# Delta rule's q, k, v projection: ten of twelve pairs of channel tiles by seven block products in place of eight, with one turning buffer

## Chip, cores and metric

One core of a Trainium2 chip runs the kernel. The metric is its device time in microseconds, the median of several executions. The other numbers come from one profiled execution of the kernel before.

## The reference

A decoder trunk of two layers over 1024 tokens of width 1024, in float32. The even layer has retention and dilated attention, the odd layer a gated delta rule; each is followed by a layer norm, a convolutional feed-forward net and another layer norm. What concerns the change is the head of the odd layer's mixer:

```python
def _odd_mixer(x, w_in, conv_w, a_log, dt_bias, norm_w, w_out):
    hproj = x @ w_in
    qkv = jax.nn.silu(_causal_dwconv(hproj[..., :3 * GDN_W], conv_w))
    gate = hproj[..., 3 * GDN_W:4 * GDN_W]
```

`3 * GDN_W` is 3072 channels: 24 tiles of 128, of which the first eight are q, then eight k, then eight v, one head each. The convolution has four taps along the tokens. The sums of squares of q and k over a head's channels are wanted later, for their lengths.

## The kernel before

All engines have queues of their own, and the order in each is written out by hand; semaphores join them. The stages follow one another on the core: `project_out` "ffn0_down" (the feed-forward net's second projection, its layer norm, and x turned to channel-major), `conv_tokens` "odd_qkv" (the stage that is changed), `project_tokens` "odd_gate", then the delta rule. Between stages all engines meet at a barrier.

**Arithmetic.** Operands are float32 numbers split in a high part (a cast, on ScalarE) and a low part (a subtraction, on VectorE). A product is three matmuls per 128 rows of contraction: high by high, high by low, low by high. x lies split in SBUF as `xhi` and `xlo`, 128 partitions by 8 channel chunks by 1024 tokens.

**`conv_tokens`, line 1834.** For each of 24 tiles, `products` (line 1881) makes 8 chunks x 3 matmuls x 2 halves of the tokens, 48 matmuls of 128x512 (line 1890), into one of two PSUM buffers. ScalarE scales the result by the last tap (line 1936), VectorE adds the other three taps straight from PSUM (line 1964), ScalarE takes the silu (line 1942). SyncE stores q and k tiles channel-major in `feat`. TensorE turns the tile by eight transposes (line 1905) into one of two turning buffers in PSUM. From there ScalarE sums the squares of q and k tiles (line 1918, eight activations) and copies k and v tiles out (line 1925) and stores them in `kv`. TensorE's queue has tile j+1's products ahead of tile j's turn. ScalarE's order for a tile is last tap, high part of tile j+2's weights (line 1914), silu, squares, copy; VectorE's is three taps, low part of tile j+2's weights (line 1955). For the last tiles `following.split_hi` and `split_lo` prepare the first weights of the gate projection.

**`ffn_up`, line 327.** The feed-forward net's first projection already works in pairs of tiles (the gate's and the value's), with 22 pairs. The first two (`PLAIN`) are made by whole products (line 470). For the other 20 the 2x2 blocks of a pair's weights (two tiles by two halves of the contraction) and of x (two halves of the contraction by two halves of the tokens) are combined so that seven block products are enough in place of eight: `product` (line 507), 12 matmuls each. VectorE makes four sums of weight blocks (`add_sources`, lines 628 to 633), ScalarE and VectorE split seven weight blocks (lines 548 and 639), and seven sums of results (lines 647 to 680) give the pair's 2x2 blocks. For this, three differences of x's blocks are made and split at the start of the stage (lines 602 to 618), and the fourth takes the place of a quarter of x in `xhi` and `xlo`. They are made from the unsplit x, which `project_out` leaves when it is given `raw` (`keep_raw`, line 890).

## Time and profile before

| | us |
|---|---|
| median of 3 runs (3083.44 to 3085.64) | 3084.43 |
| profiled execution, its own time | 3084.53 |
| its span, first to last instruction | 3082.7 |
| TensorE busy (matmuls) | 2871.6 (93%) |
| VectorE busy | 1726.1 (56%) |
| ScalarE busy | 1171.7 (38%) |
| GpSimd busy | 392.0 (13%) |
[...]

The busy shares are means over stages of different kinds. The stage that is changed runs from its first matmul at 1556.88 us to the next stage's first at 1856.22 us. In timelines a matmul's start is exact and its end modelled, so the spacing of starts tells what a matmul costs; 512 columns last 0.39 us each and follow one another faster than that. [...] In square brackets stands how long the engine had been idle before an instruction and what released it.

### The profile page before, as it was taken

How to read it: one execution, taken by the hardware profiler on the slowest of the kernel's cores; microseconds unless marked ns; L12 is line 12 of the kernel's file. 1: busy time of each engine (PE TensorE's matmuls, PEld its weight loads, DVE VectorE, ACT ScalarE, POOL GpSimd, SP SyncE). 2: the span in 40 equal slices, each digit the busy share in tenths (PEclk: the TensorE clock that was granted, in tenths of full speed). 3: DMA queues.
4: the chain of work that ended last, by engine and by line, in shares of the span. 5: the costliest groups of instructions: out<-in, count | busy, mean ns of one | idle time of the engine just before them, and what ended most of it. 6: DMA issues, size and time to landing. Idle time of an engine off the chain costs nothing. (4 is left out here: it accounts for less than half of the span.)

```text
span 3082.7 us, 45826 instructions
## 1 busy us (share of the span) xinstructions
PE 2871.6 (93%) x17734; PEld 2419.6 (78%) x17734; DVE 1726.1 (56%) x2736; ACT 1171.7 (38%) x2046; POOL 392.0 (13%) x337
## 2 busy tenths in 40 slices
PE   8999967979899999999989989799987999999996
PEld 6888856877778888788778876699976888887885
DVE  4111125674769999736544442255538799996363
ACT  3211124752344444322334532355434444443221
POOL 0000046330100000000010001255412000000002
PEclk9999988999999999999989999899998999999998
DMA  4322143425222222354322422432032222224443
GB/s 166 103 88 95 68 153 112 115 71 184 96 84 89 82 84 86 144 179 145 131 105 96 132 67 77 168 104 92 16 137 101 79 82 85 87 82 181 143 143 126
DMA packets 149994, 337.59 MB, mean 110 GB/s; under 512 B 36096, under 2 KB 70080, under 8 KB 139328
## 3 DMA queue, kind: packets, MB, share of 16 engines
q1 hardware_dynamic: 119632, 297.43, 28.4%
q10 hardware_dynamic: 30192, 37.82, 3.6%
q8 instruction: 116, 1.90, 0.3%
q14 instruction: 54, 0.44, 0.0%
HBM read 251.12 MB, written 84.05 MB: 109 GB/s over the span
## 5 line engine op out<-in xcount | busy, mean ns | idle before, releaser
L308 PE MATMUL even_in_acc<-even_in_w_hi,even_x_hi 128*128 128x512 f32 x576 | 224.9, 390 | 13.5 <-DVE even_x_lo L266 13.5
L309 PE MATMUL even_in_acc<-even_in_w_lo,even_x_hi 128*128 128x512 f32 x576 | 224.8, 390 | 0.0
L310 PE MATMUL even_in_acc<-even_in_w_hi,even_x_lo 128*128 128x512 f32 x576 | 224.8, 390 | 0.0
L272 DVE TENSOR_TENSOR even_in_w_lo<-even_in_w_raw,even_in_w_hi 128x512 fp32r<-128x512 f32 x72 | 49.6, 691 | 291.3 <-ACT even_in_w_hi L229 291.3
L1964 DVE SCALAR_TENSOR_TENSOR odd_qkv_conv<-odd_qkv_acc,odd_qkv_taps,odd_qkv_conv 128x1023 f32<-128x1023 f32 (+2 forms) x72 | 92.3, 1282 | 172.4 <-ACT odd_qkv_conv L1936 170.6
L958 DVE TENSOR_TENSOR ffn_a_lo<-ffn_a_raw,ffn_a_hi 128x512 fp32r<-128x512 f32 x84 | 58.0, 691 | 229.8 <-ACT ffn_a_hi L879 229.8
L1041 POOL TENSOR_SCALAR ffn_down_rstd<-ffn_down_mean_var 128x1 f32<-128x1 f32 x16 | 6.0, 374 | 1347.1 <-DVE ffn_down_mean_var L976 1347.1
L879 ACT CAST ffn_a_hi<-ffn_a_raw 128x512 fp32r<-128x512 f32 x84 | 52.3, 623 | 321.7 <-PE ffn_down_acc L921 310.5
L308 PEld LDWEIGHTS even_in_acc<-even_in_w_hi,even_x_hi 128*128 128x128 f32 x576 | 108.6, 189 | 35.9 <-issue 13.4
L310 PEld LDWEIGHTS even_in_acc<-even_in_w_hi,even_x_lo 128*128 128x128 f32 x576 | 108.5, 188 | 22.8
L309 PEld LDWEIGHTS even_in_acc<-even_in_w_lo,even_x_hi 128*128 128x128 f32 x576 | 108.5, 188 | 22.5
L1890 PE MATMUL odd_qkv_acc<-odd_x_hi,one_hi 128*128 128x512 f32 x384 | 121.2, 397 | 3.8 <-PEq L64 3.8
L1890 PE MATMUL odd_qkv_acc<-odd_x_lo,one_hi 128*128 128x512 f32 x384 | 119.0, 391 | 0.0
L1890 PE MATMUL odd_qkv_acc<-odd_x_hi,one_lo 128*128 128x512 f32 x384 | 118.8, 391 | 0.0
L921 PE MATMUL ffn_down_acc<-two_hi,ffn_a_hi 128*128 128x512 f32 x352 | 108.5, 390 | 3.5 <-DVEq L952 2.7
L921 PE MATMUL ffn_down_acc<-four_hi,ffn_a_hi 128*128 128x512 f32 x352 | 108.8, 391 | 2.7 <-DVEq L952 2.7
L921 PE MATMUL ffn_down_acc<-four_hi,ffn_a_lo 128*128 128x512 f32 x352 | 109.2, 392 | 0.0
L921 PE MATMUL ffn_down_acc<-four_lo,ffn_a_hi 128*128 128x512 f32 x352 | 108.9, 391 | 0.0
L921 PE MATMUL ffn_down_acc<-two_hi,ffn_a_lo 128*128 128x512 f32 x352 | 108.4, 389 | 0.0
L921 PE MATMUL ffn_down_acc<-two_lo,ffn_a_hi 128*128 128x512 f32 x352 | 108.4, 389 | 0.0
L239 ACT ACTIVATE even_in_stage<-even_in_acc 128x2048 f32<-128x2048 f32 x18 | 33.8, 1879 | 175.3 <-PE even_in_acc L310 175.3
L229 ACT CAST even_in_w_hi<-even_in_w_raw 128x512 fp32r<-128x512 f32 x72 | 44.7, 623 | 125.2 <-PE even_in_acc L310 117.7
(503 smaller groups left out, 7962.7 us busy)
## 6 DMA issues: line engine op xcount, KB each, us to landing
ffn_w_raw<-in_ffn_up SPq DMA_DIRECT2D x42, 1024.0 KB, 4.9
ffn_down_w_raw<-in_ffn_down SPq DMA_DIRECT2D x84, 512.0 KB, 3.7
ffn_a_raw<-hidden SPq DMA_DIRECT2D x88, 256.0 KB, 3.8
even_in_w_raw<-in_ev_w_in SPq DMA_DIRECT2D x18, 1024.0 KB, 5.6
hp<-even_in_stage ACTq DMA_DIRECT2D x18, 1024.0 KB, 4.2
even_out_w_raw<-in_ev_w_out SPq DMA_DIRECT2D x24, 512.0 KB, 3.6
hidden<-even_mixed SPq DMA_DIRECT2D x22, 512.0 KB, 2.6
odd_qkv_w_raw<-in_od_w_qkv SPq DMA_DIRECT2D x22, 512.0 KB, 4.3
```

The lines of the kernel that those rows point to most:

```text
L229: act.copy(at(w_hi, k), w_raw[:, k]).then_inc(hi_ready, 1)
L239: act.activation(stage[:, h], acc[:, h], func).then_inc(acc_free, 1)
L272: dve.tensor_tensor(at(w_lo, k), w_raw[:, k], f32(at(w_hi, k)), ALU.subtract).then_inc(lo_ready, 1)
L308: pe.matmul(acc[:, h, t], xhi[:, k, tok], at(w_hi, k), start=(k == 0), stop=False)
L309: pe.matmul(acc[:, h, t], xhi[:, k, tok], at(w_lo, k), start=False, stop=False)
L310: mm = pe.matmul(acc[:, h, t], xlo[:, k, tok], at(w_hi, k), start=False, stop=(k == KD - 1))
L879: act.copy(a_hi[:, s], a_part(2 * i + s, s, hf)).then_inc(hi_ready, 1)
L921: mm = pe.matmul(acc[:, t, n], aa[:, s, tok], ww[:, s, n * NB:(n + 1) * NB], start=(opening and aa is a_hi and ww is w_hi), stop=(last and ...
L958: dve.tensor_tensor(a_lo[:, s], a_part(k, s, hf), f32(a_hi[:, s]), ALU.subtract).then_inc(lo_ready, 1)
L1041: pool.tensor_scalar(rstd[:, t], mean_var[:, t, 1:2], EPS, None, ALU.add).then_inc(rstd_ready, 1)
L1890: mm = pe.matmul(acc[:, s, tok], ww[:, s, k], xx[:, k, tok], start=(k == 0 and ww is w_hi and xx is xhi), stop=(k == KD - 1 and ww is w_lo))
L1964: dve.scalar_tensor_tensor(out=conv[:, s, back:SEQ], in0=acc[:, s, 0:SEQ - back], scalar=tap(j, GDN_CONV - 1 - back), in1=conv[:, s, back: ...
```

## The change

`conv_tokens` takes over the scheme of `ffn_up`. The 24 tiles form 12 pairs; the first two pairs are made by whole products (192 matmuls), the other ten by seven block products (84 matmuls each in place of 96). The results are collected in SBUF (`c`), and the taps read them there. Six PSUM banks hold results, two hold the only turning buffer, so that a tile is turned when the tile before has been squared and copied out. The first projection's end keeps the unsplit x (`raw`), and conv, rows, c and the weight sums lie in its place later. One quarter of x is overwritten by a difference; it is stored in HBM at the start (`quarter`), loaded again after the last weights are split, and split anew for the gate projection. The gate's first weights are loaded late, into place `one`. The closing of the outer scope (`ctx.close()`) moves behind the stage. `split_hi`, `split_lo`, `add_sources`, `keep_first` and the `add_` functions are as in `ffn_up`, but that the last sum of u reuses the second's buffer.

```diff
--- before.py
+++ after.py
-def conv_tokens(nc, name, xhi, xlo, w, taps_dram, ident, n_tiles, feat, out, sumsq, first, place, following):
+def conv_tokens(nc, name, xhi, xlo, x_raw, w_raw, w, taps_dram, ident, n_tiles, feat, out, sumsq, first, places, following, quarter):
...
+    KH = KD // 2
+    PLAIN = 2
+    ORDER = 7
+    BANKS = 6
+    PAIRS = n_tiles // 2
+    W = PAIRS - PLAIN
+    LAST = PAIRS - 1
+    SUMMED = (2, 1, 3)
...
+        c, conv, rows = (x_raw[:, 2 * n:2 * n + 2] for n in range(3))
+        rows = rows.rearrange("p s (t n) -> p s t n", n=P)
+        sums = x_raw[:, 6:8].rearrange("p a (k n) -> p (a k) n", n=P).rearrange("p (i k) n -> p i k n", k=KH)
+        t_hi = sc.sbuf("t_hi", [P, 3, KH, HALF], F32R)
+        t_lo = sc.sbuf("t_lo", [P, 3, KH, HALF], F32R)
+        u1, u2, u4 = (sc.sbuf(f"u{n}", [P, HALF]) for n in (1, 2, 4))
...
-        acc = sc.psum("acc", [P, 2, SEQ])
-        turn = sc.psum("turn", [P, 2, TT, P])
+        bank = sc.psum("acc", [P, BANKS, HALF])
+        turn = sc.psum("turn", [P, TT, P])
...
+        def source(m, i):
+
+            raw = w_raw[:, m % 2]
+            return (raw[:, 0, chunks[0]], sums[:, 1], sums[:, 0], sums[:, 2], raw[:, 0, chunks[1]], sums[:, 3],
+                    raw[:, 1, chunks[1]])[i]
+
+        def operand(i):
+
+            def quarter(k, t):
+                return [x[:, chunks[k], toks[t]] for x in (xhi, xlo)]
+
+            def difference(n):
+                return [x[:, n] for x in (t_hi, t_lo)]
+
+            return (quarter(0, 0), difference(0), quarter(0, 1), difference(1), quarter(1, 0), quarter(1, 1), difference(2))[i]
+
...
+            sp.dma_start(quarter, x_raw[:, chunks[0], toks[1]]).then_inc(quarter_stored, 16)
+            load_raw(1)
             sp.dma_start(taps[:], taps_dram).then_inc(taps_in, 16)
+            load_raw(2)
+            sp.wait_ge(first_lo, 3)
+            load_raw(3)
+            for j in range(2):
+                store_feat(j)
+            for m in range(W):
+                for j in range(2 * m + 2, 2 * m + 4):
+                    store_feat(j)
+                if m + 2 < W:
+                    sp.wait_ge(lo_done, ORDER * (m + 1))
+                    load_raw(m + 4)
+            sp.wait_ge(lo_done, ORDER * W)
+            sp.wait_ge(quarter_stored, 16)
+            sp.dma_start(again, quarter).then_inc(quarter_in, 16)
+            sp.wait_ge(prod_done, ORDER * (W - 1) + 3)
+            following.load(sp)
...
+            def product(m, i):
+                pe.wait_ge(lo_done, ORDER * m + i + 1)
+                if m == 0 and i < 6:
+                    pe.wait_ge(evicted, (2, 2, 3, 3, 4, 4)[i])
+                if m > 0 and i == 0:
+                    pe.wait_ge(u2_done, m)
+                if m > 0 and i == 1:
+                    pe.wait_ge(u4_done, m)
+                if m > 0 and i == 2:
+                    pe.wait_ge(c22_done, m)
+                    pe.wait_ge(u3_done, m)
+                if m > 0 and i == 3:
+                    pe.wait_ge(c11_done, m)
+                if m > 0 and i == 4:
+                    pe.wait_ge(c12_done, m)
+                if m > 0 and i == 5:
+                    pe.wait_ge(c21_done, m)
+                if i == 6:
+                    pe.wait_ge(u1_done, m + 1)
...
+                hi, lo = operand(i)
+                for k in range(KH):
+                    for n, (ww, xx) in enumerate(((slot(0, i), hi), (slot(0, i), lo), (slot(1, i), hi))):
+                        mm = pe.matmul(result(m, i), ww[:, k], xx[:, k], start=(k == 0 and n == 0), stop=(k == KH - 1 and n == 2))
                 mm.then_inc(prod_done, 1)
...
+            def turn_tile(j):
                 pe.wait_ge(silu_done, j + 1)
-                if j > 1:
-                    pe.wait_ge(squared, TT * min(j - 1, QK))
-                if j - 2 >= Q:
-                    pe.wait_ge(copied, j - 1 - Q)
+                if j > 0:
+                    pe.wait_ge(squared, TT * min(j, QK))
...
+            low, high = range(KH), range(KH, KD)
+            pe.wait_ge(first_lo, 2)
+            for g in range(2):
+                for f in range(2):
+                    mm = whole_part(0, g, f, range(KD), True, True)
+                mm.then_inc(whole_done, 1)
+            pe.wait_ge(first_lo, 3)
+            whole_part(1, 0, 1, low, True, False)
+            whole_part(1, 0, 0, range(KD), True, True)
+            mm = whole_part(1, 0, 1, high, False, True)
+            mm.then_inc(whole_done, 1)
+            pe.wait_ge(evicted, 1)
+            mm = whole_part(1, 1, 1, low, True, False)
+            mm.then_inc(early_done, 1)
+            whole_part(1, 1, 0, range(KD), True, True)
+            mm = whole_part(1, 1, 1, high, False, True)
+            mm.then_inc(whole_done, 1)
+            turn_tile(0)
+            for m in range(W):
+                for i in range(ORDER):
+                    product(m, i)
+                    if m == 0 and i == 1:
+                        turn_tile(1)
+                    if i == (3 if m == 0 else 2):
+                        turn_tile(2 * m + 2)
+                    if i == 5:
+                        turn_tile(2 * m + 3)
+            for g in range(2):
+                turn_tile(2 * LAST + g)
...
+            def evict(j, g):
+                act.wait_ge(whole_done, 2 * j + g + 1)
+                if j == 0:
+                    act.wait_ge(t_lo_done, 3 * KH)
+                else:
+                    act.wait_ge(taps_done, g + 1)
+                act.copy(c[:, g], bank[:, (4 * j + 2 * g) % BANKS:(4 * j + 2 * g) % BANKS + 2].rearrange("p f t -> p (f t)")
...
+            def last_tap(j, g):
+                tile = 2 * j + g
+                if j < PLAIN:
+                    act.wait_ge(evicted, tile + 1)
+                elif g == 0:
+                    act.wait_ge(c11_done, j - PLAIN + 1)
+                    act.wait_ge(c12_done, j - PLAIN + 1)
+                else:
+                    act.wait_ge(c22_done, j - PLAIN + 1)
+                    act.wait_ge(c21_done, j - PLAIN + 1)
+                if j > 0:
+                    act.wait_ge(turned, tile - 1)
+                    act.wait_ge(feat_stored[g], 16 * min(j, QK // 2))
+                act.activation(conv[:, g], c[:, g], ACT.Copy, scale=tap(tile, GDN_CONV - 1)).then_inc(tap_done, 1)
+
+            def silu(tile):
+                act.wait_ge(taps_done, tile + 1)
+                act.activation(conv[:, tile % 2], conv[:, tile % 2], ACT.Silu).then_inc(silu_done, 1)
+
+            def take_rows(tile):
+                act.wait_ge(turned, tile + 1)
+                if tile < QK:
+                    for t in range(TT):
+                        act.activation(squares[:, t], turn[:, t], ACT.Square, accum_out=sumsq[:, t, tile:tile + 1]
+                                       ).then_inc(squared, 1)
+                    act.wait_ge(squared, TT * (tile + 1))
+                if tile >= Q:
+                    s, i = tile % 2, tile - Q
+                    act.wait_ge(stored[s], 16 * (i // 2))
+                    act.copy(rows[:, s], turn[:]).then_inc(copied, 1)
+                    act.wait_ge(copied, i + 1)
+                    act.dma_start(out[:, :, i * P:(i + 1) * P].rearrange("t p n -> p t n"), rows[:, s]).then_inc(stored[s], 16)
...
+            for g in range(2):
+                evict(0, g)
+            for g in range(2):
+                last_tap(0, g)
+            for g in range(2):
+                silu(g)
+            evict(1, 0)
+            act.wait_ge(early_done, 1)
+            for k in range(KH):
+                first_difference_hi(k)
+            for i in range(3):
+                split_hi(0, i)
+            evict(1, 1)
+            for i in range(3, ORDER):
+                split_hi(0, i)
+            take_rows(0)
+            last_tap(1, 0)
+            for m in range(W):
+                more = m + 1 < W
+                tile = 2 * m + 2
+                keep_first(m)
+                if m == 0:
+                    take_rows(1)
+                    last_tap(1, 1)
+                if more:
+                    split_hi(m + 1, 0)
+                silu(tile)
+                if more:
+                    for i in range(1, 3):
+                        split_hi(m + 1, i)
+                take_rows(tile)
+                if more:
+                    split_hi(m + 1, 3)
+                silu(tile + 1)
+                if more:
+                    split_hi(m + 1, 4)
+                else:
+                    act.wait_ge(quarter_in, 16)
+                    act.wait_ge(prod_done, ORDER * m + 3)
+                    act.copy(xhi[:, chunks[0], toks[1]], again).then_inc(quarter_hi, 1)
                     following.split_hi(act)
-                act.wait_ge(acc_free, j + 1)
-                act.activation(conv[:, s], conv[:, s], ACT.Silu).then_inc(silu_done, 1)
-                act.wait_ge(turned, j + 1)
-                if j < QK:
-                    square_rows(j)
-                if j >= Q:
-                    copy_out(j)
+                last_tap(m + PLAIN, 0)
+                if more:
+                    split_hi(m + 1, 5)
+                take_rows(tile + 1)
+                if more:
+                    split_hi(m + 1, 6)
+                last_tap(m + PLAIN, 1)
+            for g in range(2):
+                silu(2 * LAST + g)
...
+            dve.wait_ge(quarter_stored, 16)
+            differences(0)
+            for k in range(1, KH):
+                differences(k)
+                differences_lo(k - 1)
+                if k == 2:
+                    dve.wait_ge(first_hi, 3)
+                    dve.tensor_tensor(whole_lo[1], w_raw[:, 1], f32(whole_hi[1]), ALU.subtract).then_inc(first_lo, 1)
+            differences_lo(KH - 1)
+            dve.wait_ge(taps_in, 16)
+            for g in range(2):
+                other_taps(g)
+            for k in range(KH):
+                first_difference_lo(k)
+            split_lo(0, 0)
+            add_sources(0)
+            for i in range(1, ORDER):
+                split_lo(0, i)
+            for m in range(W):
+                more = m + 1 < W
+                tile = 2 * m + 2
+                if more:
+                    add_sources(m + 1)
+                other_taps(tile)
+                add_u2(m)
+                if more:
+                    split_lo(m + 1, 0)
+                add_u4(m)
+                if more:
+                    split_lo(m + 1, 1)
+                other_taps(tile + 1)
+                add_c22(m)
+                add_u3(m)
+                if more:
+                    split_lo(m + 1, 2)
+                    split_lo(m + 1, 3)
+                add_c11(m)
+                add_c12(m)
+                if more:
+                    split_lo(m + 1, 4)
+                    split_lo(m + 1, 5)
+                else:
+                    dve.wait_ge(quarter_hi, 1)
+                    dve.tensor_tensor(xlo[:, chunks[0], toks[1]], again, f32(xhi[:, chunks[0], toks[1]]), ALU.subtract)
                     following.split_lo(dve)
+                add_c21(m)
+                if more:
+                    split_lo(m + 1, 6)
+            for g in range(2):
...
+    quarter = dram("quarter", [P, KD // 2, HALF])
...
-            gate_first = Ahead(top, "odd_gate", two, KD // 2,
+            gate_first = Ahead(top, "odd_gate", one, KD // 2,
                                [t["od_w_gate"][0, :, 0:KD // 2].rearrange("p k n -> p (k n)")], 2)
             project_out(nc, "ffn0_down", None, KF, k_rows(t["ffn_down0"]), x1, t["ln2_g"][0:1], t["ln2_b"][0:1],
                         ident, x2, x2_hi, x2_lo, place=two, first=down_first, following=qkv_first,
-                        rows=rows, a_stored=h_stored[0], lead=rest)
+                        rows=rows, a_stored=h_stored[0], lead=rest, raw=mixed[:, 0:KD])
+            conv_tokens(nc, "odd_qkv", x2_hi, x2_lo, mixed[:, 0:KD], w_raw, t["od_w_qkv"], t["od_taps"], ident, 3 * GDN_W // P,
+                        feat, kv, sumsq, qkv_first, (one, two), gate_first, quarter)
             ctx.close()
-            conv_tokens(nc, "odd_qkv", x2_hi, x2_lo, t["od_w_qkv"], t["od_taps"], ident, 3 * GDN_W // P, feat, kv, sumsq,
-                        qkv_first, one, gate_first)
             project_tokens(nc, "odd_gate", x2_hi, x2_lo, t["od_w_gate"], GDN_W // NB, gate, None,
                            lambda sc, lent: project_decay(sc, lent, x2_hi, x2_lo, t["od_w_ba"], t["od_a_log"],
                                                           t["od_dt_bias"], upper, ident, gates, sumsq, gc_rows),
-                           ACT.Silu, gate_stored, gate_first, (two, one))
+                           ACT.Silu, gate_stored, gate_first, (one, two))
         places_ctx.close()
 
         one = weight_place(top_ctx, "three")

```

## Rows read from the trace of the kernel before

**Rows 1.** Stretches: us, busy time of each engine, TensorE's granted clock, DMA share, GB/s

```profile
1563.00:1640.00 77.00, 77.00 (x365) 64.19 (x364) 29.87 (x24) 29.58 (x98) 0.00 (x0) 1.00 0.24 83
```

**Rows 2.** Timeline of TensorE in the stage: start us, duration us, engine, line, operation

```profile
1640.10 0.71 PE L1890 MATMUL odd_qkv_acc<-odd_x_hi,one_hi 128*128 128x512 f32 x2
...
1651.87 0.70 PE L1890 MATMUL odd_qkv_acc<-odd_x_hi,one_hi 128*128 128x512 f32 x2
```

**Rows 3.** Timeline of TensorE, two products of a pair in the feed-forward stage

```profile
1000.54 0.39 PE L507 MATMUL ffn_up_tiles_acc<-ffn_x_hi,two_hi 128*128 128x512 f32 x1
...
1003.26 0.39 PE L507 MATMUL ffn_up_tiles_acc<-ffn_up_tiles_t_hi,two_hi 128*128 128x512 f32 x1
```

**Rows 4.** Timeline of VectorE, feed-forward stage, then the taps in the changed stage

```profile
1000.74 0.69 DVE L680 TENSOR_TENSOR even_mixed<-ffn_up_tiles_acc,ffn_up_tiles_u 128x512 f32<-128x512 f32 x1 [0.83 <-PE ffn_up_tiles_acc L507]
1001.40 0.69 DVE L639 TENSOR_TENSOR one_lo<-ffn_w_raw,one_hi 128x512 fp32r<-128x512 f32 x1
1002.01 0.69 DVE L628 TENSOR_TENSOR even_mixed<-ffn_w_raw 128x512 f32<-128x512 f32 x1
...
1004.54 1.27 DVE L423 SCALAR_TENSOR_TENSOR even_mixed<-even_mixed,ffn_up_taps 128x1023 f32<-128x1023 f32 x1
...
1643.74 3.92 DVE L1964 SCALAR_TENSOR_TENSOR odd_qkv_conv<-odd_qkv_acc,odd_qkv_taps,odd_qkv_conv 128x1023 f32<-128x1023 f32 x3 [6.75 <-ACT odd_qkv_conv L1936]
```

**Rows 5.** Timeline of ScalarE, feed-forward stage, then silu and a k tile's rows

```profile
908.73 0.61 ACT L548 CAST one_hi<-even_mixed 128x512 fp32r<-128x512 f32 x1
909.24 0.62 ACT L548 CAST one_hi<-ffn_w_raw 128x512 fp32r<-128x512 f32 x1
...
1001.52 1.24 ACT L414 ACTIVATE even_mixed<-even_mixed,ffn_up_taps 128x1024 f32<-128x1024 f32 x1 [0.15 <-DVE even_mixed L680]
...
1647.69 1.06 ACT L1942 ACTIVATE odd_qkv_conv<-odd_qkv_conv 128x1024 f32<-128x1024 f32 x1 [3.05 <-DVE odd_qkv_conv L1964]
...
1699.31 0.28 ACT L1918 ACTIVATE odd_qkv_squares<-odd_qkv_turn 128x128 f32<-128x128 f32 x1 [1.56 <-PE odd_qkv_turn L1905]
...
1701.52 1.02 ACT L1925 COPY odd_qkv_rows<-odd_qkv_turn 128x1024 f32<-128x1024 f32 x1
...
1703.06 1.12 ACT L1936 ACTIVATE odd_qkv_conv<-odd_qkv_acc,odd_qkv_taps 128x1024 f32<-128x1024 f32 x1 [0.52 <-ACT odd_qkv_rows L1925]
```

**Rows 6.** Timeline of TensorE, from first turn to the next stage, with and without keep_raw

```profile
831.73 2.78 PE L947 MATMUL even_out_acc<-top_ident,even_out_y 128*128 128x128 f32 x24
...
859.73 0.76 PE L470 MATMUL ffn_up_tiles_acc<-ffn_x_hi,two_hi 128*128 128x512 f32 x1 [4.23 <-PEq L64]
...
1529.60 2.79 PE L947 MATMUL ffn_down_acc<-top_ident,ffn_down_y 128*128 128x128 f32 x24
...
1556.88 1.19 PE L1890 MATMUL odd_qkv_acc<-odd_x_hi,one_hi 128*128 128x512 f32 x2 [3.77 <-PEq L64]
```

**Rows 7.** DMA issues of the page: line, count, KB each, us from issue to landing

```profile
hp<-even_in_stage ACTq DMA_DIRECT2D x18, 1024.0 KB, 4.2
```

**Rows 8.** Instructions of line 507: count, ns min/median/max, first and last start

```profile
L507 PEld LDWEIGHTS ffn_up_tiles_acc<-ffn_x_hi,two_hi x160: 187/188/188, 905.1 to 1274.4; 128*128 128x128 f32 x160
```

**Rows 9.** Timeline of TensorE, the end of the stage

```profile
1839.72 1.04 PE L1905 MATMUL odd_qkv_turn<-top_ident,odd_qkv_conv 128*128 128x128 f32 x8
1848.53 1.97 PE L1905 MATMUL odd_qkv_turn<-top_ident,odd_qkv_conv 128*128 128x128 f32 x8 [7.78 <-ACT odd_qkv_conv L1942]
1856.22 0.76 PE L308 MATMUL odd_gate_acc<-two_hi,odd_x_hi 128*128 128x512 f32 x1 [5.72 <-DVEq L276]
```

**Rows 10.** Matmuls after gaps (TensorE's timeline), and one stretch as in group 1

```profile
673.48 1.06 PE L1664 MATMUL dil_bank<-top_ident,dil_probs 128*128 128x128 f32 x8 [1.19 <-ACT dil_probs_t L1715]
...
1288.95 0.70 PE L921 MATMUL ffn_down_acc<-two_hi,ffn_a_hi 128*128 128x512 f32 x2 [2.65 <-DVEq L952]
...
2815.40 0.70 PE L921 MATMUL ffn_down_acc<-four_hi,ffn_a_hi 128*128 128x512 f32 x2 [2.70 <-DVEq L952]
...
2818.00:2820.00 2.00, 2.00 (x6) 1.55 (x6) 2.00 (x2) 0.77 (x1) 0.00 (x0) 0.56 0.94 307
```

224 lines of the change are left out of this document (151 added, 73 removed).

## The prediction

> **What bounds the kernel now.** I read the stretches first, to see whether the stage that is edited is held by TensorE. It is: TensorE is busy in all 77.00 us of the stretch, at a granted clock of 1.00, while VectorE and ScalarE are busy for 30 us each [rows 1]. Then the order in time. One tile of the projection takes 11.77 us from its first product to the next tile's (1640.10 to 1651.87) [rows 2]. Forty-eight matmuls of 128x512 fill most of it; the feed-forward stage, which already uses seven block products, shows their spacing: 12 in 2.72 us (1000.54 to 1003.26), 0.2267 us each [rows 3]. That makes 10.88 us, and leaves 0.89 us for the tile's eight transposes. So matmuls that are taken out here are worth their full time, as long as the other two engines keep up. The profiled execution took 3084.53 us (span 3082.7); the sum is made against that, 0.1 us above the median of 3084.43.
>
> **What is removed.** Ten pairs go from 96 matmuls to 84. A pair then takes 84 x 0.2267 + 2 x 0.89 = 20.82 us of TensorE in place of 23.54 [rows 2, 3]: 2.72 us a pair, 27.2 us in all, if nothing waits.
>
> **What VectorE gets.** A pair costs it: six taps, 2 x 3.83 us (three in 3.92 us; the last overlaps its successor) [rows 4]; four sums of weights, 2.53 us (1002.01 to 1004.54); seven low parts and seven sums of results at about 0.61 us (1001.40 to 1002.01), 8.5 us. Together 18.7 of 20.82 us. It is not the bound by its sum. The order in its queue is another matter.
>
> **The walk through one pair.** Let T be the start of a pair's first product. Products are 2.72 us, so TensorE wants the first of the pair's two turns (the transposes of one tile) after three of them, at T+8.16. That turn waits for the tile's silu, which waits for its taps, which stand in VectorE's queue behind the four sums of the next weights, which stand behind the last low part of the pair's own weights, and this waits for ScalarE's last high part. In the feed-forward stage that high part comes at once. Here `take_rows` of the other tile stands ahead of it, and with one turning buffer that tile is turned only after the sixth product.
> From the end of the sixth product of the pair before, then: results are visible 0.20 us later (1000.54 to 1000.74), their sum takes 0.69, and ScalarE starts the tap 0.09 us after its end (1001.52) [rows 4, 5]. On ScalarE: tap 1.14 us (it lasts 1.24, and overlaps its successor by 0.1 as the high parts do, 0.61 long and 0.51 apart), high part 0.52 [rows 5], `take_rows`, last high part 0.62 and 0.04 to VectorE. `take_rows` is 2.21 us for q tiles (squares, 1699.31 to 1701.52), 1.54 for v tiles (copy, and its store's issue, to 1703.06), 3.75 for k tiles, which do both [rows 5]. On VectorE: low part 0.61, sums 2.53, taps 3.92 [rows 4]; silu 1.09 with its start, 0.05 to TensorE. Without `take_rows` that is 0.98+1.14+0.52+0.66+0.61+2.53+3.92+1.14 = 11.50 us. TensorE has 0.89+2.72+8.16 = 11.77 us of own work between the same two points (one turn, the seventh product, three products). So the wait of the first turn is `take_rows` minus 0.27: 1.9 us after a q tile, 3.5 after a k tile, 1.3 after a v tile. It recurs in each pair, since the chain starts from TensorE's own sixth product and so moves with the wait.
> Now count. The second to the tenth pair have this chain. The second starts behind a fuller VectorE: in the first pair two tiles' taps follow each other late (the walk from the head gives its last low part at T+3.15 in place of T+1.9, a wait of 3.1). The third and fourth follow q tiles (2 x 1.9), the fifth to eighth k tiles (4 x 3.5), the ninth a v tile (1.3); the tenth has no next weights to sum, its taps begin 2.5 us sooner, no wait. Sum: **22.2 us** given back of 27.2. A pair behind a k tile takes 24.3 us, more than the 23.54 of before.
>
> **Head.** `keep_raw` adds eight copies out of PSUM on ScalarE to the end of the projection before, and TensorE's last turns wait for them. From the first turn to the next stage's first matmul it took 27.28 us without them (1529.60 to 1556.88) and 28.00 with them (831.73 to 859.73): +0.7 [rows 6]. Closing the outer scope, which moves behind the stage, I take as 0.6 at the end, bounds 0 and 1.5.
> The store of x's quarter is new and VectorE's first difference waits for it. It is 1024 KB; such a store took 4.2 us to land [rows 7]. SyncE's queue has the weights of the second pair behind it, which are needed only after TensorE's first 96 matmuls, over 20 us later. All of VectorE's and ScalarE's head moves by some 5 us. In the walk the differences end at 25 us, silu of the second tile at 37, when TensorE is at 37 itself; the second weights of the first seven-product pair are split at 44.4 and wanted at 48.9. So the store costs nothing with 4.5 us to spare. Its bounds are 0 and the 5 us of it that are not covered if it lands twice as late.
> The four plain tiles took 45.4 us in the feed-forward stage (859.73 to 905.1) [rows 6, 8], the slow first matmuls included; same work here. One turn (0.89), then the first pair with three turns, 21.71.
>
> **Tail.** Now 16.50 us pass from the last product's end to the next stage's first matmul (1839.72 to 1856.22) [rows 9]. After: both last tiles must be tapped, silued, turned at the slow rate (1.97 us for eight, row 1848.53) and copied one after the other, 4.6 us for store and barrier as now. What VectorE does ahead: the quarter's low part (128x2048, about 2.2 us) and the next weights' low parts (4 x 0.61) stand before the last sum, which starts 1.7 us late. Then 7.8 us of taps, silu 1.1, turn 2.0, copy 1.0: 19.8 us, +3.3. The quarter's load is issued at T+1.5 of the last pair and read at T+14, so it is hidden.
>
> **Sum.** Stage after: 45.4 + 0.9 + 21.7 + 9 x 20.82 + 22.2 + 19.8 + 0.6 = 298.0 us; before 1556.88 to 1856.22, 299.3; with 0.7 at the head the change is **-0.6 us**.
>
> **The clock.** What is new is that TensorE stands still in the middle of dense matmuls, for 2.9 us once, 3.3 us four times (the wait less the 0.16 us in which the last matmul drains). The trace has few such gaps: 2.65 us was followed by full speed (two matmuls in 0.70, then pairs 0.54 apart), 2.70 us by a clock of 0.56 in the stretch 2.6 us later, and 1.19 by full speed [rows 10]. The two rows near 2.7 are the same place in the two layers, the start of the down projection, and went both ways; 3.3 is longer than either. Bounds for one gap: nothing, and 1.9 us, which is what the slow start of the feed-forward stage cost (45.4 us for 192 matmuls that make 43.5 at 0.2267). I take 1.5 for each of the five: **+7.5 us**. The waits after q tiles (gap 1.75) lie between 1.19 and 2.65: 0 each, up to 1.7.
> [...]
> So 3084.53 - 0.6 + 7.5 = 3091.4 us.
>
> **Rivals.** What a measurement can tell from no change is 0.2%, 6.2 us.
> A, the walk with the clock falling: 3091.4, from 3087 to 3095. Chance 0.50.
> B, the walk, and the clock holds or falls while the engine stands anyway: -0.6, some 3084. For it the 2.65 us row [rows 10], against it the 2.70 us row. 0.15.
> C, ScalarE's and VectorE's chain is shorter than the walk (an order that I read too strictly, steps that overlap more), and the silus come in time: -0.6 - 22.2 = -22.8, some 3062. For it: both engines have time to spare by their sums; against: every step has its row and the queues run in order. 0.15.
> D, slower: the clock falls at every wait of the first turn, and and stays down twice as long behind the k tiles, where the engine stands longest. 3 x 1.7 for the q and v waits, 4 x 1.9 more for the k waits: 3104. It decides if the gap of 1.75 us is enough; nothing between 1.19 and 2.65 in my rows says no. 0.20.
> That the matmuls do not become fewer can be excluded: the loops give 192 + 840 in place of 1152.
>
> **Numbers.** A lies about the bound of 3090.6: 0.32 slower, 0.18 same. B: 0.12 same, 0.03 faster. C faster, D slower. Faster 0.18, same 0.30, slower 0.52. The range reaches from below B, a third of the way to C, to near D: 3074 to 3103.
>
> **What would show it.** In the changed profile: 84 matmuls and two turns in 20.8 us where nothing waits; TensorE idle ahead of the first turn of pairs two to nine, released by ScalarE's silu, longest behind k tiles; VectorE's last low part released by ScalarE, not by TensorE; a granted clock under 1 several times in the stage. Wrong would be: no idle before the turns (C), or a clock of 1.00 throughout (B), or a first seven-product pair that waits for VectorE's splits (the store is not hidden).

## The result and the profile after

The changed kernel takes 3092.98 us (median of 13 runs, 3089.28 to 3097.37), the kernel before, beside it, 3085.37 us (13 runs, 3082.09 to 3092.2): ratio 1.0024, 95% interval 1.0015 to 1.0032. It is slower, by a little more than the 0.2% that the prediction took as the least that can be told from no change. Its profiled execution took 3092.21 us, with a span of 3090.4. Of the 7.7 us by which that span is longer, the profile has 1.0 ahead of the stage, 3.8 in it, and 2.9 behind it, in code that is the same.

The page of the changed kernel, busy time of each engine:

```profile
span 3090.4 us, 46057 instructions
PE 2853.5 (92%) x17614; PEld 2401.6 (78%) x17614; DVE 1836.2 (59%) x2928; ACT 1216.8 (39%) x2134; POOL 393.4 (13%) x337
```

TensorE has 120 matmuls fewer and is busy 18.1 us less, but VectorE works 110 us more and ScalarE 45. The same stretch as in [rows 1], after:

```profile
1563.00:1640.00 77.00, 74.17 (x342) 61.66 (x341) 66.06 (x87) 45.75 (x123) 0.00 (x0) 0.98 0.24 89
```

VectorE was busy for 29.87 of 77 us and now is for 66.06. The stage is no longer TensorE's alone: TensorE idles in it, and its granted clock (a share of full speed, the mean over the stretch) is 0.98 in place of 1.00. Where it idles stands in its timeline. These rows are the first turn of the projection before, the stage's first matmul, its first turn, and then turns before which TensorE waited, two of them with the pair's other turn below:

```profile
1529.72 2.78 PE L947 MATMUL ffn_down_acc<-top_ident,ffn_down_y 128*128 128x128 f32 x24
...
1557.86 0.76 PE L1959 MATMUL odd_qkv_acc<-odd_x_hi,one_hi 128*128 128x512 f32 x1 [4.35 <-PEq L64]
...
1603.15 1.03 PE L2000 MATMUL odd_qkv_turn<-top_ident,even_mixed 128*128 128x128 f32 x8
...
1636.98 1.97 PE L2000 MATMUL odd_qkv_turn<-top_ident,even_mixed 128*128 128x128 f32 x8 [2.83 <-ACT even_mixed L2086]
...
1661.09 1.09 PE L2000 MATMUL odd_qkv_turn<-top_ident,even_mixed 128*128 128x128 f32 x8 [1.65 <-ACT even_mixed L2086]
...
1708.03 1.92 PE L2000 MATMUL odd_qkv_turn<-top_ident,even_mixed 128*128 128x128 f32 x8 [3.14 <-ACT even_mixed L2086]
...
1733.83 1.09 PE L2000 MATMUL odd_qkv_turn<-top_ident,even_mixed 128*128 128x128 f32 x8 [3.09 <-ACT even_mixed L2086]
1742.95 1.03 PE L2000 MATMUL odd_qkv_turn<-top_ident,even_mixed 128*128 128x128 f32 x8
...
1758.00 1.09 PE L2000 MATMUL odd_qkv_turn<-top_ident,even_mixed 128*128 128x128 f32 x8 [3.12 <-ACT even_mixed L2086]
1768.75 1.04 PE L2000 MATMUL odd_qkv_turn<-top_ident,even_mixed 128*128 128x128 f32 x8
...
1848.13 1.97 PE L2000 MATMUL odd_qkv_turn<-top_ident,even_mixed 128*128 128x128 f32 x8 [7.27 <-ACT even_mixed L2086]
...
1860.99 0.77 PE L308 MATMUL odd_gate_acc<-one_hi,odd_x_hi 128*128 128x512 f32 x1 [6.32 <-DVEq L276]
```

The seven-product pairs wait 2.83 us once, 1.65 and 1.67 behind q tiles, 3.14, 3.09, 3.12 and 3.12 behind k tiles, 0.89 behind a v tile, and the last not at all. Each wait is released by ScalarE's silu (line 2086). A clock that fell can be read off the rows without a view of the clock: from the waiting turn to the pair's other turn it is 9.12 us after the 3.09 us gap (1733.83 to 1742.95) and 10.75 after the next (1758.00 to 1768.75), for the same work. The stretches of 4 us behind three of these turns have it as a granted clock of 0.57, 1.00 and 0.67:

```profile
1708.00:1712.00 4.00, 3.97 (x15) 3.49 (x16) 3.93 (x6) 3.02 (x18) 0.00 (x0) 0.57 0.34 135
1733.00:1737.00 4.00, 3.17 (x18) 2.80 (x19) 3.96 (x6) 3.85 (x19) 0.00 (x0) 1.00 0.35 135
1758.00:1762.00 4.00, 4.00 (x16) 3.32 (x17) 3.93 (x6) 3.81 (x19) 0.00 (x0) 0.67 0.33 131
```

And this is the chain behind one such wait, ScalarE first, then VectorE (a high part and then the eight squares of the k tile stand where ScalarE's first "..." is):

```profile
1719.75 1.15 ACT L2082 ACTIVATE even_mixed<-even_mixed,odd_qkv_taps 128x1024 f32<-128x1024 f32 x1 [2.87 <-DVE even_mixed L2236]
...
1723.52 1.02 ACT L2098 COPY even_mixed<-odd_qkv_turn 128x1024 f32<-128x1024 f32 x1
1724.57 0.37 ACTq L2100 DMA_DIRECT2D kv<-even_mixed  x1
1724.98 0.62 ACT L2061 CAST two_hi<-ffn_w_raw 128x512 fp32r<-128x512 f32 x1 [0.44 <-ACT even_mixed L2098]
...
1732.72 1.06 ACT L2086 ACTIVATE even_mixed<-even_mixed 128x1024 f32<-128x1024 f32 x1 [5.08 <-DVE even_mixed L2249]
```

```profile
1718.98 0.69 DVE L2236 TENSOR_TENSOR even_mixed<-odd_qkv_acc,odd_qkv_u 128x512 f32<-128x512 f32 x1 [2.03 <-PE odd_qkv_acc L1990]
...
1725.63 0.69 DVE L2203 TENSOR_TENSOR two_lo<-ffn_w_raw,two_hi 128x512 fp32r<-128x512 f32 x1 [2.32 <-ACT two_hi L2061]
1726.24 0.69 DVE L2192 TENSOR_TENSOR even_mixed<-ffn_w_raw 128x512 f32<-128x512 f32 x1
...
1728.77 3.91 DVE L2249 SCALAR_TENSOR_TENSOR even_mixed<-even_mixed,odd_qkv_taps 128x1023 f32<-128x1023 f32 x3
```

The other tile's rows hold ScalarE from 1721.32 to 1724.94, so the last high part comes at 1724.98; VectorE waits 2.32 us for it, then sums the next weights, and only then taps the tile that TensorE wants. The changed kernel run again on another chip gave the same picture.

> The changed kernel once more, for the comparisons of this call. About 1.0024 of the kernel before (some 7.6 us over it). Walk: the eight waits before a pair's first turn come again, 20.8 us in all, 1.8 us after q tiles and 3.3 us after k tiles; the clock falls after some of the gaps of about 3 us, not the same ones each time, so single times differ by multiples of some 1.5 us.

Measured: 3092.7 us, ratio 1.0020 (1.0011 to 1.0029). The waits are 2.83, 1.66, 1.66, 3.13, 3.09, 3.12, 3.12 and 0.91 us, within 0.02 us of the first profile; the clock fell after three of the five long ones, not after four (the granted clock of the 4 us from the turn is 0.59, 0.57 and 0.65 after the three, 1.00 after the other two).

### The profile page after: what moved, and what is told of

The parts are those of the page before. It is cut to its first block and busy times, and to the rows that moved or that the text cites. A ratio compares the mean times of both kernels' runs of the same rounds, so it can differ in the third digit from the quotient of the medians.

```text
span 3090.4 us, 46057 instructions
## 1 busy us (share of the span) xinstructions
PE 2853.5 (92%) x17614; PEld 2401.6 (78%) x17614; DVE 1836.2 (59%) x2928; ACT 1216.8 (39%) x2134; POOL 393.4 (13%) x337
## 5 line engine op out<-in xcount | busy, mean ns | idle before, releaser
L2249 DVE SCALAR_TENSOR_TENSOR even_mixed<-even_mixed,odd_qkv_taps 128x1023 f32<-128x1023 f32 (+2 forms) x72 | 92.1, 1281 | 4.9 <-ACT even_mixed L2082 3.2
L921 PEld LDWEIGHTS ffn_down_acc<-two_hi,ffn_a_hi 128*128 128x128 f32 x352 | 66.5, 189 | 19.1 <-DVEq L952 3.0
L921 PEld LDWEIGHTS ffn_down_acc<-four_hi,ffn_a_hi 128*128 128x128 f32 x352 | 66.5, 189 | 17.3 <-DVEq L952 3.3
L2676 PE MATMUL gdn_bank<-gdn_xt_blk,gdn_t_m 64*64 64x64 f32 x1280 | 78.7, 221 | 0.8 <-DVE gdn_t_m L2913 0.8
```

What stands on the lines that cost most here:

```text
L921: mm = pe.matmul(acc[:, t, n], aa[:, s, tok], ww[:, s, n * NB:(n + 1) * NB], start=(opening and aa is a_hi and ww is w_hi), stop=(last and ...
L2249: dve.scalar_tensor_tensor(out=conv[:, g, back:SEQ], in0=c[:, g, 0:SEQ - back], scalar=tap(tile, GDN_CONV - 1 - back), in1=conv[:, g, back ...
L2676: pe.matmul(d_ps[q][half, h % HG], t_m[half, h], xt_blk[half, s, h], start=True, stop=True)
```

## The experiments

**The chain, cut on ScalarE.**

```diff
-                take_rows(tile + 1)
                 if more:
                     split_hi(m + 1, 6)
+                take_rows(tile + 1)
```

> ScalarE makes the last high part of the next weights before it takes the other tile's rows out of the turning buffer. Walk (the rows stand ahead of that high part, and so ahead of VectorE's sums, taps and the silu): the wait before the first turn becomes the same after q, k and v tiles, 0.9 us each (1.6 for the second pair), 7.9 us in all in place of 20.8; no gap is over 2 us, so the clock stays at full speed: about 19 us under the changed kernel, some 3074. Rival 1, the single turning buffer holds TensorE: rows are taken out later than before, so the same or longer, 3093 or more. Rival 2, VectorE is short of time as a whole (18.7 of 20.8 us): within 3 us of 3093.

Measured: 3075.63 us, ratio 0.9959 (0.9945 to 0.9972). The wait behind a k tile in this kernel's timeline:

```profile
1703.69 1.09 PE L2000 MATMUL odd_qkv_turn<-top_ident,even_mixed 128*128 128x128 f32 x8 [0.73 <-ACT even_mixed L2086]
```

The waits are 1.47 us once and then 0.73 or 0.74 seven times, behind q, k and v tiles alike, and the clock fell nowhere between the head and the tail (granted 1.00 from 1610 to 1824 us). So what made the waits differ by kind of tile was `take_rows` ahead of the last high part. One swap takes the ratio from 1.0020, on the same chip, to 0.9959: the gaps add up to 6.6 us in place of 19.5, and the falls of the clock are gone as well.

**The chain, cut on VectorE.**

```diff
-                if more:
-                    add_sources(m + 1)
                 other_taps(tile)
+                if more:
+                    add_sources(m + 1)
```

> VectorE adds the first tile's taps before it sums the next pair's weight blocks. Walk: the chain to the silu is 2.5 us shorter; waits only in the second pair (0.6 us) and the four pairs behind k tiles (0.8 each), 3.8 us in all in place of 20.8, no fall of the clock: about 23 us under the changed kernel, some 3070. Rival 1, the single turning buffer: no difference, since the rows are taken out at the same time. Rival 2, VectorE short of time: no difference, since its work is the same.

Measured: 3078.81 us, ratio 0.9975 (0.9966 to 0.9985): faster, but 9 us short of the expectation. The waits are 1.23 (new: the first pair's second turn), 0.85, 0.55, 0.54, 2.01, 2.00, 2.00 and 0.59 us. VectorE's timeline in a pair of k tiles shows why:

```profile
1690.50 0.68 DVE L2236 TENSOR_TENSOR even_mixed<-odd_qkv_acc,odd_qkv_u 128x512 f32<-128x512 f32 x1
...
1697.15 0.69 DVE L2203 TENSOR_TENSOR two_lo<-ffn_w_raw,two_hi 128x512 fp32r<-128x512 f32 x1 [2.90 <-ACT two_hi L2061]
1697.76 3.92 DVE L2249 SCALAR_TENSOR_TENSOR even_mixed<-even_mixed,odd_qkv_taps 128x1023 f32<-128x1023 f32 x3
1701.59 0.69 DVE L2192 TENSOR_TENSOR even_mixed<-ffn_w_raw 128x512 f32<-128x512 f32 x1
```

I had taken 2.5 us off each wait. But the four sums are only moved: they now stand between the taps and the sixth result's sum (line 2236), which starts straight behind its predecessor, held by VectorE, where it had waited 2.03 us for TensorE. The chain starts later, and `take_rows` is still in it (2.90 us for the high part). The clock fell after one of the three gaps of 2.0 us (granted 0.58 in the 4 us from the turn, 1.00 after the other two), and here that was nearly free: the wait after it is 0.59 us in place of 2.00, and from this waiting turn to the next it is 23.27 us against 23.06 without a fall.

**Both cuts.**

> Both orders together. Walk: no wait before any turn, TensorE without a gap from the stage's first product to the last pair's end; 20.8 us and the clock's 6 us come back: about 27 us under the changed kernel, some 3066, 0.6% under the kernel before. Rival 1 and rival 2: as with one order alone, 3090 or more.

Measured: 3068.28 us, ratio 0.9936 (0.9922 to 0.9949). From the second pair on no turn waits. The middle of the stage, this kernel first and the changed one below it:

```profile
1642.00:1820.00 178.00, 174.63 (x839) 145.55 (x837) 157.74 (x199) 112.49 (x290) 0.00 (x0) 1.00 0.39 128
```

```profile
1642.00:1820.00 178.00, 161.32 (x746) 132.98 (x745) 137.64 (x177) 100.19 (x277) 0.00 (x0) 0.97 0.32 107
```

In 178 us there are 839 matmul records instead of 746, at a clock of 1.00 instead of 0.97. The stage takes 277.7 us in place of 303.1: the 25.4 us between them are the 20.8 of waits and some 6 of clock, less the 1.21 us that the first pair's second turn now waits.

**The clock apart from the wait.** Eleven extra matmuls, whose results nobody reads, fill most of each of the five long gaps (m = 1, 4, 5, 6, 7):

```diff
+                    if i == 2 and m in (1, 4, 5, 6, 7):
+                        pe.wait_ge(lo_done, ORDER * m + 4)
+                        pe.wait_ge(c11_done, m)
+                        for _ in range(11):
+                            pe.matmul(result(m, 3), slot(0, 3)[:, 0], operand(3)[0][:, 0], start=True, stop=True)
                     if i == (3 if m == 0 else 2):
                         turn_tile(2 * m + 2)
```

> As the changed kernel, but in the five pairs with a gap of about 3 us (the second, the fifth to eighth) TensorE fills the wait before the first turn with 11 matmuls of 128x512 whose results the next product overwrites: 2.5 us of work, done before the silu comes. Walk and clock: the turns start when they did, the eight waits cost the same 20.8 us, but the granted clock stays at 1.00 from the stage's first turn to its last pair, which takes away three or four falls of 1.6 us: 5 to 6 us under the changed kernel, some 3087. Rival: the clock falls for another reason (the load of the whole kernel), and then the falls stay, and the time is 3093; or the added matmuls delay the turns, and then it is above.

Measured: 3088.19 us, ratio 1.0011 (1.0001 to 1.0020).

```profile
1703.39 2.65 PE L2030 MATMUL odd_qkv_acc<-odd_qkv_t_hi,two_hi 128*128 128x512 f32 x11
1706.68 1.09 PE L2000 MATMUL odd_qkv_turn<-top_ident,even_mixed 128*128 128x128 f32 x8 [0.63 <-ACT even_mixed L2091]
```

The eleven take 2.65 us, the turn comes when it did, and the k pairs still follow each other at 24.17 us. Four gaps of 0.62 or 0.63 and one of 0.35 are left, and the granted clock is 1.00 from 1610 to 1835 us. The stage is 5.3 us shorter (297.8 against 303.1). Its first turn comes 0.7 us later here than in the changed kernel (46.0 us into the stage against 45.3), and from that turn on it is 6.0 us shorter, as much as the four falls cost by the rows. Idling thus cost the waits themselves and, on top, some 6 us of clock: the two terms are separate, as the sum had them.

**The quarter of x.** Its store, its load and its new split are left out here, so the gate projection reads the difference in that quarter's place:

```diff
-            sp.dma_start(quarter, x_raw[:, chunks[0], toks[1]]).then_inc(quarter_stored, 16)
...
-            sp.dma_start(again, quarter).then_inc(quarter_in, 16)
...
-                    act.copy(xhi[:, chunks[0], toks[1]], again).then_inc(quarter_hi, 1)
...
-            dve.wait_ge(quarter_stored, 16)
...
-                    dve.wait_ge(quarter_hi, 1)
-                    dve.tensor_tensor(xlo[:, chunks[0], toks[1]], again, f32(xhi[:, chunks[0], toks[1]]), ALU.subtract)
```

> Leaves out that x's quarter is stored, loaded again and split again, so the gate projection works on a wrong quarter of x. Walk: VectorE starts its differences 7.5 us sooner, and no product starts sooner for it (0 us in the stage's head); at the end VectorE's last sum starts as soon as TensorE's last product is done, and the two last tiles come 1.7 us sooner: 3091, 2 us under the changed kernel. Rival: the store holds up the head, and then the first turn or the first products of the first seven-product pair come sooner too, by up to 5 us: 3086.

Measured: 3090.78 us, ratio 1.0021 (1.0012 to 1.0031). In the changed kernel VectorE's first difference waits for the store:

```profile
1563.37 0.69 DVE L2167 TENSOR_TENSOR even_mixed<-even_mixed 128x512 f32<-128x512 f32 x1 [7.55 <-DMA quarter<-even_mixed]
```

Here it starts 5.5 us after the stage's first matmul (1557.86), without the store at once (1560.19, where the first matmul starts too). Yet the first turn that waits comes 79.1 us into the stage with the store (1636.98) and 78.9 without: hidden. At the tail the last tiles' first turn waits 5.70 us in place of 7.27, which looks like the quarter's low part that stood ahead of the last sum. The next run has the same 5.70 with that part still there.

**The tail alone.**

```diff
-                    following.split_lo(dve)
                 add_c21(m)
...
             for g in range(2):
                 other_taps(2 * LAST + g)
+            following.split_lo(dve)
```

> The changed kernel with the end of the stage altered alone: the last sum is made before the gate projection's low part, which goes behind the last taps. Theory: the tail's last sum was 1.7 us late because of that low part and the end of the stage follows the last sum through the last taps, silu and turn, so the wait before the last tile's first turn falls from 7.3 to about 5.6 us and the kernel takes 1.6 us less: 3091. Rival: the gate projection then waits for the low part that now comes last, and nothing is gained: 3092.7; or the low part lands behind the taps inside the last silu and is hidden.

Measured: 3091.61 us, ratio 1.0019 (1.0010 to 1.0028). The trace has the expected 1.6 us (first row), and the gate projection waits for nothing more (second row, 6.32 us as above); the times can't tell 1.6 us from nothing.

```profile
1851.45 1.97 PE L2000 MATMUL odd_qkv_turn<-top_ident,even_mixed 128*128 128x128 f32 x8 [5.70 <-ACT even_mixed L2086]
1864.31 0.77 PE L308 MATMUL odd_gate_acc<-one_hi,odd_x_hi 128*128 128x512 f32 x1 [6.32 <-DVEq L276]
```

The last sum on VectorE's timeline, in the changed kernel, without the quarter, and with the tail's order:

```profile
1837.26 0.69 DVE L2236 TENSOR_TENSOR even_mixed<-odd_qkv_acc,odd_qkv_u 128x512 f32<-128x512 f32 x1 [2.04 <-PE odd_qkv_acc L1990]
1837.87 2.28 DVE L2297 TENSOR_TENSOR odd_x_lo<-even_mixed,odd_x_hi 128x2048 fp32r<-128x2048 f32 x1
1840.07 2.49 DVE L119 TENSOR_TENSOR one_lo<-one_raw,one_hi 128x512 fp32r<-128x512 f32 x4
1842.48 0.68 DVE L2241 TENSOR_TENSOR even_mixed<-odd_qkv_acc,odd_qkv_u 128x512 f32<-128x512 f32 x1
```

```profile
1842.81 0.69 DVE L2234 TENSOR_TENSOR even_mixed<-odd_qkv_acc,odd_qkv_u 128x512 f32<-128x512 f32 x1 [0.54 <-PE odd_qkv_acc L1986]
```

```profile
1845.79 0.69 DVE L2241 TENSOR_TENSOR even_mixed<-odd_qkv_acc,odd_qkv_u 128x512 f32<-128x512 f32 x1 [0.75 <-PE odd_qkv_acc L1990]
```

With both blocks ahead of it (4.6 us together) the sum starts without a wait, late; with either one gone it waits for TensorE's last product. There was room for one block, not for two: the 1.6 us belong to neither alone. Since the sum then waits for TensorE, taking both away should bring no more; no run did.

**One turning buffer, in the kernel before.** Its second buffer taken away (`turn` of [P, TT, P], each turn waiting for the tile ahead of it), nothing else.

> The kernel before, with the one part alone that the turning buffer is single. Walk: a tile's rows are taken out within 3.8 us of its turn, and the next turn comes 11.8 us later, so nothing waits and the time is that of the kernel before within 0.1%. Rival (the single buffer is what costs in the changed kernel): TensorE waits for ScalarE's squares or copies ahead of turns, 10 us or more over.

Measured: 3085.11 us, ratio 1.0002 (0.9993 to 1.0011); the stage takes 299.4 us against 299.3. One buffer costs nothing by itself. That in the changed kernel it holds `take_rows` back, on an engine that something urgent is queued on, was only argued: no run there has two. What is shown is that the place of `take_rows` in ScalarE's queue costs.

**The raw parts of x, in the kernel before.** `raw=mixed[:, 0:KD]` added to the call of `project_out`; the outer scope closes ahead of the projection, as it did.

> The kernel before, with the one part alone that the projection ahead leaves the unsplit x (eight copies out of PSUM on ScalarE). From that projection's first turn to the changed stage's first matmul 28.0 us in place of 27.3, the rest as before: 0.7 us over the kernel before, which the median can't show and the trace can. Rival: the copies are not hidden, 8 us over.

Measured: 3090.17 us, ratio 1.0019 (1.0010 to 1.0028), a miss: 5.6 us where 0.7 was expected. The trace had only 2.2 of it in the head, the stretch from the first turn to the stage's first matmul, and 0.2 in the stage. The kernel was run again, beside one in which the scope closes behind the projection, as in the change:

```diff
-            ctx.close()
             conv_tokens(nc, "odd_qkv", x2_hi, x2_lo, t["od_w_qkv"], t["od_taps"], ident, 3 * GDN_W // P, feat, kv, sumsq,
                         qkv_first, one, gate_first)
+            ctx.close()
```

> The same kernel as the earlier run with the raw parts kept and the scope closed ahead of the projection, beside the run with the scope closed late on the same chip. Theory that its 5.6 us were mostly scatter from one chip to another: the head is 29.5 us again and the ratio near 1.0007 (2.2 us). Rival: they are the kernel's own: ratio 1.0019 again.

> The kernel before with two of the change's parts: the raw residual halves kept in the even layer's buffer while ffn0_down's rows are turned, and the scope of that buffer closed behind the q, k, v projection in place of ahead of it. Against the run with the raw parts kept and the scope closed ahead (ratio 1.0019, first turn to first product 29.5 us against 27.3 before). Theory: keeping the raw parts costs 0.7 us and the closing of a scope whose buffer was just written costs the rest of the 2.2 us, so here the head is 28.0 us, as in the changed kernel, and the ratio 1.0002 to 1.0005. Rival: the raw parts cost all of it wherever the scope closes: head 29.5, ratio 1.0019 as there. Second rival: the time behind the stage, in which 3 us accrued in unchanged code, comes with the raw parts: head 28.0, ratio 1.0013 or more.

Measured: 3087.93 us, ratio 1.0010 (1.0001 to 1.0019), with the scope closed ahead, and 3089.26 us, ratio 1.0008 (0.9999 to 1.0018), with it closed behind. Their last eight turns and first products, scope closed ahead and then behind:

```profile
1551.72 1.97 PE L947 MATMUL ffn_down_acc<-top_ident,ffn_down_y 128*128 128x128 f32 x8 [1.08 <-POOL ffn_down_y L1056]
1558.49 1.19 PE L1890 MATMUL odd_qkv_acc<-odd_x_hi,one_hi 128*128 128x512 f32 x2 [4.80 <-PEq L64]
```

```profile
1533.15 2.78 PE L947 MATMUL ffn_down_acc<-top_ident,ffn_down_y 128*128 128x128 f32 x24
...
1555.83 1.09 PE L947 MATMUL ffn_down_acc<-top_ident,ffn_down_y 128*128 128x128 f32 x8 [1.14 <-POOL ffn_down_y L1056]
1561.28 1.19 PE L1890 MATMUL odd_qkv_acc<-odd_x_hi,one_hi 128*128 128x512 f32 x2 [4.35 <-PEq L64]
```

From the first turn to the product it is 28.13 us with the scope closed behind (1533.15 to 1561.28), the same as in the changed kernel (1529.72 to 1557.86), with a last gap of 4.35 us; closed ahead, the gap is 4.80. But these two differ in another thing as well, and so does the row that I compared in the prediction. The last eight turns took either 1.97 us, at a granted clock of 0.50, or 1.09, at 1.00. Here they are, from the kernel before, ahead of the feed-forward stage and ahead of the changed one (the first turns and products of both stand in [rows 6]), from the same with one turning buffer, and from the changed kernel:

```profile
854.41 1.09 PE L947 MATMUL even_out_acc<-top_ident,even_out_y 128*128 128x128 f32 x8 [1.07 <-POOL even_out_y L1056]
...
1551.14 1.97 PE L947 MATMUL ffn_down_acc<-top_ident,ffn_down_y 128*128 128x128 f32 x8 [2.07 <-POOL ffn_down_y L1056]
```

```profile
1530.85 2.79 PE L947 MATMUL ffn_down_acc<-top_ident,ffn_down_y 128*128 128x128 f32 x24
...
1552.39 1.10 PE L947 MATMUL ffn_down_acc<-top_ident,ffn_down_y 128*128 128x128 f32 x8 [2.07 <-POOL ffn_down_y L1056]
1557.26 1.19 PE L1890 MATMUL odd_qkv_acc<-odd_x_hi,one_hi 128*128 128x512 f32 x2 [3.77 <-PEq L64]
```

```profile
1552.42 1.09 PE L947 MATMUL ffn_down_acc<-top_ident,ffn_down_y 128*128 128x128 f32 x8 [1.13 <-POOL ffn_down_y L1056]
```

| head, first turn to first product | last turns 1.09 us | last turns 1.97 us |
|---|---|---|
| no raw parts, scope closed ahead (before) | 26.41 | 27.28 |
| raw parts, scope closed behind (the change) | 28.13 | 29.01 |
| raw parts, scope closed ahead | not seen | 29.44 |

Of the ten profiles with a head of the second row, four have 28.1 and six 29.0. Like beside like, the change makes the head 1.7 us longer. That is 2.2 us for keeping the raw parts (29.44 against 27.28), less 0.4 because the scope no longer closes there. The closing costs as much at its new place. These are the gate projection's first matmuls, scope closed ahead and then behind:

```profile
1858.22 0.77 PE L308 MATMUL odd_gate_acc<-two_hi,odd_x_hi 128*128 128x512 f32 x1 [5.72 <-DVEq L276]
```

```profile
1861.11 0.77 PE L308 MATMUL odd_gate_acc<-two_hi,odd_x_hi 128*128 128x512 f32 x1 [6.19 <-DVEq L276]
```

The gap is 0.5 us longer with the scope closed behind, so moving the closing gains nothing. What is left of the first run's 5.6 us did not come again (it had 1229.7 us from the gate projection's start to the end of the span, the second 1226.8). The head's 2.2 us make a ratio of 1.0007: the second run's interval (1.0001 to 1.0019) holds it, the first one's (1.0010 to 1.0028) does not, and was too narrow for the scatter. The theory is right that the closing costs something and wrong in how much; the ratios of the two kernels can't be told apart.

**The best order.** Both cuts, the sums ahead of the taps kept in the first pair alone, and the tail's order.

```diff
-                if more:
+                if more and m == 0:
                     add_sources(m + 1)
                 other_taps(tile)
+                if more and m > 0:
+                    add_sources(m + 1)
```

> The changed kernel with three orders altered: the next pair's last high part ahead of the second tile's last turns on ScalarE, the first tile's taps ahead of the next sums on VectorE from the second pair on (the first pair keeps the changed kernel's order, because there the sums ahead of the taps cost nothing), and at the end the last sum ahead of the gate projection's low part. Against the kernel with the first two orders everywhere (3068.3 us) two things are left to gain: the 1.2 us for which TensorE there waited before the second turn of the first pair, and 1.7 us by which the low part stood ahead of the last sum at the stage's end. Theory that each wait is worth its length: 3065.5 us, ratio to before 0.9935 or just below. Rival: the first pair's wait only moves to the second pair's first turn, as in the run with the high part moved alone (1.47 us there), and the tail is set by the turns and their silu: 3068.

Measured: 3067.96 us, ratio 0.9942 (0.9929 to 0.9956).

```profile
1821.78 1.97 PE L2000 MATMUL odd_qkv_turn<-top_ident,even_mixed 128*128 128x128 f32 x8 [5.70 <-ACT even_mixed L2086]
```

This is now the first turn of the stage that waits at all. The stage takes 274.8 us against 277.7 with the two cuts alone: both waits are gone by their full length. In the medians (3067.96 against 3068.28) it can't be seen. Both versions beat the kernel before by about 0.6%; which of them is faster the times leave open.

## Why the prediction came out right

**What is removed, and the waits.** Right, by its steps. Forecast and measured: waits 22.2 and 20.8 us in all (the gaps of the trace, 19.5, and 0.16 us each for the draining matmul, as the prediction counts it); period behind a k tile 24.3 and 24.17 (1733.83 to 1758.00), behind a q tile 22.7 and 22.74; the pair without next weights, none and none. The difference is mostly 0.2 us less in each k pair's chain, and then the wait behind the v tile (1.05 with the drain, 1.3 forecast). The reason stood the test: the order of ScalarE's queue makes the difference between tiles, the order of VectorE's the rest, and without both TensorE runs through at 20.86 us a pair (forecast 20.82). Rival C is refuted by the same rows.

**Head.** Here a term was mis-sized: 0.7 us was forecast, and like beside like the change adds 1.7, the raw parts' 2.2 less the 0.4 of the scope's closing. The step compared 27.28 us, whose last turns ran at a granted clock of 0.50, with 28.00, whose last turns ran at 1.00 [rows 6]; the last turns' own rows, 1551.14 and 854.41 above, would have said so. The profile of the change happened to have fast ones, so its head is only 0.9 us longer. The scope's closing at the stage's end: forecast 0.6, the author's estimate, which no row of the kernel before shows, with bounds 0 and 1.5; measured 0.5 (6.19 against 5.72). The quarter's store landed 5.5 us after the stage's start rather than 4.2, within its bounds and hidden. The first turn came 45.3 us into the stage (forecast 45.4).

**Tail.** From the last product's end (about 1840.7) to the gate projection 20.3 us, against 19.8 and 0.6 forecast and 16.5 before. That low parts delay the last sum by 1.7 us is shown by two runs (1.6 us each).

**The clock.** The sign was right, the size a little high: 7.5 forecast for five falls; four falls of 1.3 to 1.6 us make 6.0. In the three other profiles with these waits, three falls make 4.8 to 5.8 us. The bound of 1.9 us for one gap was too low: two falls cost 2.8. And behind the gap of 2.65 us in [rows 10] the pairs are 0.54 us apart once and then 0.45 to 0.47, at a granted clock of 1.00 all the same (1288.90 to 1293.00). Rival B (the clock holds) is refuted: with the gaps filled the stage was 5.3 us shorter. Rival D (the clock falls at every wait) too: the gaps of 1.65 and 1.67 never cost anything (granted 1.00 in the 4 us behind each), and the falls behind k tiles stayed at 1.3 to 1.6 us.

**The sum.** Stage forecast 298.0 + 7.5 = 305.5, measured 303.1. The total, 3091.4 forecast and 3092.98 measured, came nearer than its parts: what the stage took less, the 2.9 us of the unchanged code behind it made up. Over the 14 profiles of this study that part, the same code in all, ranges from 1226.1 to 1232.6 us. A forecast of 3091.4 can't claim to be better than these 6 us, and a single profile's total can't either; differences inside the stage repeat to 1 or 2 us.

## What to carry to other kernels

Fewer instructions on the bounding engine are worth their time only if the others deliver at the new pace, and that is decided by the order in their queues, not by their busy share: ScalarE was free for 60% of the span, and the other tile's squares and copy ahead of a 0.6 us cast cost 12.9 us of waits and the clock's 6 on top. When a scheme is taken from one stage to another, walk the loop once around, from TensorE's result back to TensorE's next need, with what the new stage adds to each queue; whatever does not feed that loop goes behind what does. Moving a block out of one wait puts it somewhere else in the same queue: look which instruction is then late.

## What the runs showed of the hardware

**Gaps and the clock.** In the four profiles that have the changed kernel's waits, the clock fell after each gap of 2.83 to 2.85 us (four of four), but after only 9 of 16 gaps of 3.08 to 3.14. With the cut on VectorE three gaps of 2.0 us cost one fall; in these pairs gaps of 1.67 and below never cost one. So the length of the gap alone does not decide, and the falls after equal gaps differ from one execution to the next. A fall cost 1.3 to 1.6 us in 11 of 14 cases. In two, in the second pair, it cost 2.8: with the tail's order it is 11.96 us from that pair's waiting turn to its other turn (1642.08 to 1654.04) in place of 9.14, and the granted clock is 0.50 from 1642 to 1648 us. One, with the cut on VectorE, was made up but for 0.2 us by a shorter wait after it.

**A store with loads behind it.** The 1024 KB store of x's quarter was issued at 1557.83 and released VectorE at 1563.37, 5.5 us later, where such stores took 4.2 in [rows 7]. That the loads issued right behind it are the cause was not tried.

**One piece of code, two lengths.** The head of the stage took 0.87 us more or less from one execution to the next, in kernels that are the same there, by whether its last eight turns took 1.97 us, at a granted clock of 0.50, or 1.09, at 1.00. Transitions are to be compared with a look at the clock of their last instructions.
